# The end of a mixture-of-experts kernel: held loads, lower rows on another engine, an earlier turn, two stores moved

## The reference, cut to what matters

```python
def moe_swiglu(x, router_w, w1, w3, w2):
    logits = (xt @ router_w).astype(jnp.float32)
    top_vals, top_idx = lax.top_k(logits, TOP_K)
    gates = jax.nn.softmax(top_vals, axis=-1)
    combine = jnp.sum(jax.nn.one_hot(top_idx, N_EXPERTS, dtype=jnp.float32) * gates[..., None], axis=1)
    for e in range(N_EXPERTS):
        out = out + combine[:, e:e + 1] * swiglu(xt, w1[e], w3[e], w2[e])

    h = h + moe_swiglu(f, router_w[j], moe_w1[j], moe_w3[j], moe_w2[j])
    gate = jax.nn.sigmoid(rmsnorm(h, ple_norm_g[i]) @ ple_gate_w[i])
    h = h + gate * (p[i] @ ple_proj_w[i])
```

## Time and profile before

| | us |
|---|---|
| median of 3 runs (lowest, highest) | 1708.97 (1707.74, 1710.74) |
| the profiled execution | 1711.69 |
| its span, first to last instruction | 1709.8 |
| PE busy in it (8555 products) | 1695.3 |
| DVE busy | 1378.6 |
| ACT busy | 1231.2 |
| POOL busy | 59.2 |

### The profile page before, as it was taken

One profiled execution on the slowest core, in us unless ns is written; L12 is line 12 of the kernel. 1 busy time (PEld: TensorE's weight loads), 2 busy tenths in 40 slices (PEclk: granted clock), 3 DMA queues, 4 the chain that ended last, 5 costly groups with the idle time before them and its releaser, 6 DMA issues.

```text
span 1709.8 us, 24926 instructions
## 1 busy us (share of the span) xinstructions
PE 1695.3 (99%) x8555; PEld 1415.4 (83%) x8555; DVE 1378.6 (81%) x1607; ACT 1231.2 (72%) x1564; POOL 59.2 (3%) x43
## 2 busy tenths in 40 slices
PE   9999999999999999999999999999999999999998
PEld 7877779898888889888888888888888888888786
DVE  5667876777774577699899898899898998989995
ACT  6667665665553566887888887887877878878775
POOL 0002100000000000000000000000000000000301
PEclk9999999999999999999999999999999999999999
DMA  9942354369645453299999999999999999999993
GB/s 320 345 182 95 110 193 172 123 227 419 247 179 215 154 203 148 105 393 380 373 397 372 376 386 372 379 397 365 385 386 376 388 375 370 402 370 386 380 375 123
DMA packets 76948, 510.60 MB, mean 299 GB/s; under 512 B 8312, under 2 KB 8440, under 8 KB 19537
## 3 DMA queue, kind: packets, MB, share of 16 engines
q1 hardware_dynamic: 67792, 479.45, 72.3%
q0 software_dynamic: 6496, 25.52, 4.6%
q10 hardware_dynamic: 2592, 4.72, 0.7%
HBM read 485.02 MB, written 24.64 MB: 298 GB/s over the span
## 4 chain that ended last, share of the span: by engine, by line
PE 94%; DVE 2%; DMA 1%; ACT 1%; issue 1%; ACTq 0%; SPq 0%; POOL 0%; DVEq 0%; POOLq 0%
PE ps L1990 23%; PE ps L1995 22%; PE ps L1991 22%; PE ps L2397 6%; PE ps L1954 4%; PE ps L2404 3%; PE ps L2376 1%; PE ps L2375 1%; PE ps L2382 1%; PE ps L1983 1%; PE ps L1975 1%; PE ps L1979 1%; DVE wlo L1271 1%; DMA raw<-in_w_fixed_dram 1%; PE ps L2291 1%
## 5 line engine op out<-in xcount | busy, mean ns | idle before, releaser
L1271 DVE TENSOR_TENSOR wlo<-raw,whi 128x1024 fp32r<-128x1024 f32 x886 | 1028.1, 1220 | 130.3 <-ACT whi L760 129.2
L760 ACT ACTIVATE whi<-raw 128x1024 fp32r<-128x1024 f32 x886 | 882.4, 1053 | 119.5 <-PE ps L1995 84.6
L1990 PE MATMUL ps<-whi,xgh 128*128 128x512 f32 x896 | 353.6, 395 | 0.0
L1991 PE MATMUL ps<-whi,xgl 128*128 128x512 f32 x896 | 348.9, 389 | 0.0
L1995 PE MATMUL ps<-wlo,xgh 128*128 128x512 f32 x896 | 276.7, 390 | 1.6 <-DVE wlo L1271 1.5
L1995 PEld LDWEIGHTS ps<-wlo,xgh 128*128 128x128 f32 x896 | 167.9, 188 | 38.2 <-DVE wlo L1271 2.8
L1990 PEld LDWEIGHTS ps<-whi,xgh 128*128 128x128 f32 x896 | 168.3, 188 | 34.2 <-ACT whi L760 0.4
L1991 PEld LDWEIGHTS ps<-whi,xgl 128*128 128x128 f32 x896 | 168.4, 188 | 33.4
L1990 PE MATMUL ps<-whi,mTh 128*128 128x512 f32 x448 | 175.9, 393 | 0.0
L1991 PE MATMUL ps<-whi,mTl 128*128 128x512 f32 x448 | 174.4, 389 | 0.0
L1995 PE MATMUL ps<-wlo,mTh 128*128 128x512 f32 x448 | 138.1, 389 | 0.0
(11 more groups left out here) (418 smaller groups left out, 1952.6 us busy)
## 6 DMA issues: line engine op xcount, KB each, us to landing
raw<-in_w_moe_dram SPq DMA_DIRECT2D x336, 1024.0 KB, 7.2
raw<-in_w_fixed_dram SPq DMA_DIRECT2D x112, 1024.0 KB, 5.1
tokens_scratch<-zeros POOLq DMA_DIRECT2D x1, 8704.0 KB, 44.6
y_scratch<-zeros POOLq DMA_DIRECT2D x2, 2304.0 KB, 57.6
y_scratch<-yo ACTq DMA_DIRECT2D x18, 256.0 KB, 6.0
xin<-tokens_scratch SPq DMA_DIRECT2D x8, 512.0 KB, 7.3
bias_scratch<-revb POOLq DMA_DIRECT2D x1, 3072.0 KB, 38.1
raw<-in_w_fixed_dram SPq DMA_DIRECT2D x4, 512.0 KB, 4.6
```

What stands on the lines that cost most here:

```text
L760: AC(whi[:, v % SPL, c], raw[:, v % RAW, c], ACT.Copy).then_inc(high_done, 1)
L1271: V.tensor_tensor(wlo[:, v % SPL, c], raw[:, v % RAW, c], whi[:, v % SPL, c].bitcast(F32), ALU.subtract).then_inc(low_done, 1)
L1990: mm(o, hi(k0 + k, T), wh[:, k, :], start=first and k == 0, stop=False)
L1991: mm(o, lo(k0 + k, T), wh[:, k, :], start=False, stop=False)
```

## The change

Loads: SP waits, behind the last expert's loads, until the two fetches of the left output half have landed, and then issues the four loads of the last stage. Lower rows: POOL fetches them as before, but DVE scales and adds them, in one instruction for each 128 tokens, behind the splits of units 35 and 36 of the last expert; `low_added` now counts DVE's own two instructions. Zero rows: POOL stores row block 0 of both arrays, from its zeros, together with the other cleared rows in the first layer's dense feed-forward; ACT raises the two semaphores with an increment instead of a store. Last stage: DVE adds the right half's upper rows before it splits unit 2, and its low parts of the turned right half before it splits unit 3. PE takes unit 1 in the order with `norm` and does the second turn ahead of the last four products of that unit; the four products that nobody reads are gone.

```diff
@@ SP
             g.r = rounds
             g.post = True
+            sp.wait_ge(y_fetched[0], 32)
             for j, unit in enumerate(after):
                 load(U["ple1"] + j, unit)
@@ POOL
                         pool.dma_start(y_dram[half][NE:2 * NE + 1].rearrange("a p n -> p a n"),
                                        zeros[:, 0:NB].unsqueeze(1).broadcast_to([P, NE + 1, NB]))\
                             .then_inc(rows_cleared, 16)
+                        pool.dma_start(y_dram[half][0:1].rearrange("a p n -> p (a n)"), zeros[:, 0:NB])\
+                            .then_inc(rows_cleared, 16)
...
-            pool.wait_ge(rows_cleared, 48)
+            pool.wait_ge(rows_cleared, 80)
...
                     fetch(0, T, half, y_low, low_fetched)
-            pool.wait_ge(low_fetched, 64)
-            for T in range(NT):
-                ins = pool.tensor_scalar(y_low[:, T, :], y_low[:, T, :], gk[:, 0, T:T + 1], None, ALU.mult)
-            ins.then_inc(low_scaled, 1)
-            pool.wait_ge(low_scaled, 1)
-            pool.tensor_tensor(h[:], h[:], y_low[:], ALU.add).then_inc(low_added, 1)
             pool.wait_ge(dispatched, 64)
@@ ACT
-            act.wait_ge(y_copied, 2)
             for half in range(2):
-                store(half, 0)
+                act.sem_inc(rows_stored[half], 16)
@@ DVE, expert
                 else:
+                    for T in range(NT):
+                        dve.wait_ge(low_fetched, 64)
+                        V.scalar_tensor_tensor(out=h[:, T, :], in0=y_low[:, T, :], scalar=gk[:, 0, T:T + 1],
+                                               in1=h[:, T, :], op0=ALU.mult, op1=ALU.add).then_inc(low_added, 1)
+                        split_to(ub + 4 * NFB + 6 + T + AHEAD)
                     split_to(ub + UNITS_ROUND - 1)
-                    dve.wait_ge(low_added, 1)
+                    dve.wait_ge(low_added, 2)
                     add_last(0)
@@ DVE, last_ple
+                add_last(1)
                 split_to(ub + 2)
-                add_last(1)
+                turned_low(6, 1)
                 split_to(ub + 3)
-                turned_low(6, 1)
                 invert_root(6)
@@ PE, products
                             for T, o in enumerate(outs):
                                 mm(o, hi(k0 + k, T), wl[:, k, :], start=False, stop=False)
+                        if half and before_low:
+                            before_low()
                         pe.wait_ge(low, n_parts)
@@ PE, last_ple
-                products(ub + 1, KU, NB, *X, 0, outs[1], True, False)
-                second_rows()
-                for _ in range(4):
-                    mm(ps[:, 6, :], order[:, 1, :], whi[:, (ub + 1) % SPL, 0:NB], start=True, stop=True)
+                products(ub + 1, KU, NB, *X, 0, outs[1], True, False, norm=6, before_low=second_rows)
                 products(ub + 2, KU, NB, *X, KU, outs[0], False, True, norm=6)
```

More of the change, by code:

```diff
@@ L360, in build @@
         low_fetched = sem("low_fetched")
-        low_scaled = sem("low_scaled")
         low_added = sem("low_added")
@@ L777, in root @@
                 if k == 3:
-                    act.wait_ge(rows_cleared, 48)
+                    act.wait_ge(rows_cleared, 80)
                 for i in range(NT):
@@ L1630, in mix @@
                 if i:
-                    dve.wait_ge(rows_cleared, 48)
+                    dve.wait_ge(rows_cleared, 80)
                 if i == 0:
@@ L1959, in split_view, with products @@
                         wlo[:, s, 0:nk * n].rearrange("p (k n) -> p k n", k=nk))
-            def products(u, nk, n, hi, lo, k0, outs, first, last, middle=None, halves=(0, 1), norm=None):
+            def products(u, nk, n, hi, lo, k0, outs, first, last, middle=None, halves=(0, 1), norm=None,
+                         before_low=None):
                 wh, wl = split_view(u, nk, n)
```

## The result

The changed kernel takes 1714.07 us, the kernel before 1710.45 us in the same comparison (medians of 18 runs each); the ratio is 1.0021, 95% interval 1.0015 to 1.0027. One run of the changed kernel (2094.90 us) and one of e1 further down (1797.37 us) lie far off the others and are left out of the ratios. The profiled execution took 1714.12 us, its span 1712.0 us, which is 2.2 us more than the span of before. So the change costs, where the forecast had a balance.

The account below looks back on a forecast made before the run. TensorE was taken as the bound, losing time where it stands still. A second turn 2.6 us later, less 0.85 and 1.80, gave -0.05 us: 1711.65 as profiled, 1708.9 us at the median, 8-in-10 range 1704.8 to 1713.4.

Parts of the forecast that it names:

- a balance: Whole change: two stalls won and given back through the held loads, -0.05 us in sum.
- Gains, 2.65 us: Before the last stage: 0.85 us from dropping ACT's zero stores, 1.80 us from moving the lower rows off POOL.
- The cover of DVE's additions: Last expert: DVE's pause and slack absorb most of the added 2.7 us, about 0.8 left, none reaching PE.
- The hold's chain: Last stage: loads issued at 1671.7, units in at 1676.6 and 1678.95, then ACT's splits, turned_high and copy_result(1) at 1682.85.
- The second fetch: Right output half: 7.0 us from fetch to rows, taken from the earlier trace, so rows at 1693.3.
- The balance without the clock: Second turn at 1694.9 instead of 1692.29, +2.6 us, against gains of 0.85 and 1.80; clock at 1.00.
- The clock: Last 30 us: granted clock stays 1.00; as a rival, PE's standing lowers it, +1.9 us, 1710.8 us, chance 0.20.
- The wait of about 3 us that was forecast for the second turn: Last stage: PE reaches the second turn at 1691.8 and waits 3.1 us, until 1694.9.
- the 3.8 us of standing: Before the last stage: PE, done at about 1678.0, stands until turned_high's first quarter at 1681.8.
- a hold that gains the fetch little: Rival, first fetch: rows in at 1676.2 as before, each later step 4.5 us later, 1713.4 us, chance 0.12.
- the store landing sooner: Rival, first store: without the held loads it lands about 3.2 us sooner, 1705.7 us, chance 0.12.
- the 0.05 of the forecast: Whole change: the forecast's net gain, +2.6 us at the second turn less 0.85 and 1.80.

Follow-up runs that it names:

- e1: The changed kernel plus 24 products that nobody reads, put into PE's wait ahead of the last stage: 1712.35 us, 1.0010 of the kernel before.
- e6: The kernel before with only the hold of all four last-stage loads added: 1713.07 us, 1.0019 of the kernel before.
- e5: The changed kernel with only units 2 and 3 held and DVE's two additions four units earlier: 1704.98 us, 0.9969 of the kernel before.
- e10: The changed kernel without any hold and with DVE's two additions four units earlier: 1709.44 us, 1.0005 of the kernel before.
- e2: The changed kernel with DVE's two additions behind the splits of units 31 and 32: 1710.54 us, 1.0002 of the kernel before.
- e3: The changed kernel without the wait that holds the four loads: 1708.81 us, 0.9990 of the kernel before.
- e4: The changed kernel with only the loads of units 2 and 3 held: 1706.46 us, 0.9982 of the kernel before.
- e7: The changed kernel with ACT doing turned_high and copy_result(1) before splitting units 0 and 1: 1712.86 us, 1.0017 of the kernel before.
- e8: The kernel before with only the lower rows scaled and added by DVE instead of POOL: 1710.41 us, 1.0007 of the kernel before.
- e9: The changed kernel with ACT reordered to do turned_high and copy_result(1) first, and DVE turned_low first: 1710.80 us, 1.0011 of the kernel before.

## Why the prediction failed, step by step

*Gains, 2.65 us: right.* 2.40 us by the store at 1656.30: 1.81 for the lower rows as said, 0.59 or a little more where I took 0.85 for the zero stores.

*The cover of DVE's additions: right for PE, wrong for POOL.* PE lost nothing by them. But I asked only who waits for DVE, and named no price for what runs beside it. I took the first fetch's issue over from before, 2.09 us; with DVE's pause gone it was 6.59. This term was mis-sized by 4.5 us. With a store that landed 0.7 us earlier and a second issue 1.0 us shorter, the rows came 2.8 us later than forecast on the same clock (1672.08 against 1671.7 - 2.40). So PE stood 6.34 us and not 3.8. The step behind the issue was right: from its end, 1669.48, the rows took 2.6 us, as forecast.

*The hold's chain: right.* Unit 0 split 4.94 us after the release (4.9 forecast), unit 1 2.45 later (2.35), splits 2.00 (2.01), copy to fetch 3.47 (3.46). ACT did stand waiting for the loads, as said.

*The second fetch: mis-sized the other way.* From fetch to rows 4.83 us, not the 7.0 of the earlier trace rows: DVE was idle, and both issues took 0.95 us where before they took 3.17 and 0.94.

*The balance without the clock: nearly right.* The rows were added by 1692.56, so that the second turn could have come near 1692.7; the forecast, moved by the 2.40 us, is 1692.5. Two wrong terms cancelled, which is luck.

*The clock: the step that failed.* The forecast had the clock at 1.00 through the last 30 us and gave the fall, as a rival, a chance of 0.20. It fell, PE's 44 products ended at 1694.54, and the second turn was 1.8 us late by PE, not by its rows: the rival's 1.9 us, for its reason. The wait of about 3 us that was forecast for the second turn did not come, since PE was the later one. e1 shows the cause, and e6 shows that the 3.8 us of standing that I had forecast was enough for it. The Trainium skill, "TensorE: Matmul & The Clock Gate", section "HAM oscillation — how this bites in real kernels", describes a kernel in which each wait of some 3 to 5 us for a transfer between groups of products brings the clock down. The 6.34 us here agree with that. Its example has no shorter waits; here the 2.28 us of the kernel before left the clock up, and waits of 2.23 to 2.93 us in other runs did not.

The other rivals: a hold that gains the fetch little is refuted by e5 against e10; the store landing sooner would have saved 3.2 us, but from the left half's store to its fetch it took 5.3 us in the changed kernel, 6.7 in e2 and 7.9 in e5, all with loads held, and 6.1 in the kernel before (from 1658.70, to 1664.75).

*The whole distance.* The forecast was 1708.9 us, with 1704.8 to 1713.4 as the wide range; the measured median is 5.2 us above it. Of these, 1.5 us lie in the starting point: 1708.97 was the median of three runs of the kernel before, and 18 runs gave 1710.45. The other 3.6 us are the change, with an interval from 2.6 to 4.6. The spans of the two profiled executions differ by 2.2 us, and the steps above account for that: 1.8 for the clock and 0.45 for smaller gains and later rows, less the 0.05 of the forecast. The medians differ by about 1.2 more than the profiled executions, because that of the kernel before lies 1.2 us above its own median (1711.69 against 1710.45) and that of the changed kernel does not. Why it does is not shown, so about a third of the 3.6 us stays without a cause.

## What to carry to other kernels

When a transfer is held back for another one's sake, ask of each held piece what stands behind its consumer in every engine's program order, and hold only those that are not needed next: two of these four gained, the other two cost more. When work moves to an engine with slack, its neighbours may have lived on that slack; look at what runs beside it, not only at who waits for it. And price a stall of PE also with the products after it at half clock, as a possible cost.

## What the runs showed of the hardware

**POOL's fetch issue ends with DVE's burst.** With the additions behind units 35 and 36 the splits form one stretch, and POOL's first issue ended 0.36 to 0.38 us before that stretch did: 1668.22 against 1668.60 in the changed kernel; likewise in e1, e3, e4, e7, e8 and e9, with issues of 5.50 to 6.59 us. In the second half, beside an idle DVE, an issue took 0.95 us. The Trainium skill, "SBUF — State Buffer", section "Who interferes with whom", says that a DVE instruction with two SBUF inputs contends with a GpSimd instruction that reads SBUF; the fetch reads its row numbers there, and the runs agree. That the shared port is the mechanism is not shown by them. The same section infers that such subtractions don't hold up the writing of descriptors; here the issue as a whole was held up.

**The clock is not told by the length of a wait.** It fell behind waits of 2.23 us (e7, e9), 2.44 (e8), 2.72 (e3), 2.93 (e10) and more, and stayed at 1.00 behind 2.28 in the kernel before. In e1, e7 and e9, whose edits lie in the last 60 us, it was also 1.00 from 718 to 720, where the earlier trace rows has 0.50. These three profiled executions are 1.6 to 1.9 us faster than the medians of their kernels. So one execution's clock row is an example, and not a price list, and two traces are better compared stretch by stretch than by their spans.
